# Norm seams of a two-layer hybrid backbone worked in two parts of tokens

## What is computed

```python
def _pre(x, g, mod, k):
    return _rmsnorm(x, g) * (1.0 + mod[:, 3 * k + 1][:, None]) + mod[:, 3 * k][:, None]
def _post(x, y, g, mod, k, weight):
    return x + weight * mod[:, 3 * k + 2][:, None] * _rmsnorm(y, g)
for l in range(DEPTH):
    x = _post(x, _swiglu(_pre(x, g[0], mod_lat, 0), ffn1_gu[l], ffn1_down[l]), g[1], mod_lat, 0, 0.5)
    h = _pre(x, g[2], mod_lat, 1) @ w_in[l]
    ...                                     # state-space heads and Fourier heads
    x = _post(x, y, g[3], mod_lat, 1, 1.0)
    x = _post(x, _swiglu(_pre(x, g[4], mod_lat, 2), ffn2_gu[l], ffn2_down[l]), g[5], mod_lat, 2, 0.5)
```

## Time and profile before

| | us |
|---|---|
| median of three runs (2838.31 to 2845.07) | 2840.49 |
| the profiled execution | 2843.31 |
| its span, first to last instruction | 2841.4 |
| PE busy in the span | 2729.4 |
| DVE busy | 1678.4 |
| POOL busy | 820.6 |
| ACT busy | 717.2 |

### The profile page before, as it was taken

The page is one execution under the profiler, slowest core; times in us unless marked ns, Lnnn a source line. Parts: engine busy times, 40 slices in busy tenths (PEclk is TensorE's granted clock), DMA queues, the critical chain, the costliest instruction groups (busy, mean ns, idle before and its releaser), DMA issues.

```text
span 2841.4 us, 40710 instructions
## 1 busy us (share of the span) xinstructions
PE 2729.4 (96%) x17042; PEld 2554.1 (90%) x17042; DVE 1678.4 (59%) x2235; ACT 717.2 (25%) x977; POOL 820.6 (29%) x1292
## 2 busy tenths in 40 slices
PE   5999999999999999999999899999999999999997
PEld 4899999999879899999999799999999868788886
DVE  5868876875582586766765643343344694644444
ACT  4221221112423431111111321212112424422222
POOL 1248776641050200000000226757651041100001
PEclk9899999999999999999999999999999999999999
DMA  9433444443445134344342232222323466233321
GB/s 316 126 127 129 146 137 149 125 168 98 142 149 166 52 104 127 99 131 127 110 128 82 75 72 82 90 90 86 97 86 104 162 172 191 62 97 97 97 89 60
DMA packets 340462, 337.16 MB, mean 119 GB/s; under 512 B 52528, under 2 KB 311224, under 8 KB 336696
## 3 DMA queue, kind: packets, MB, share of 16 engines
q1 hardware_dynamic: 279224, 204.07, 24.5%
q10 hardware_dynamic: 51840, 77.07, 8.1%
q0 software_dynamic: 9216, 53.42, 5.0%
HBM read 290.02 MB, written 44.50 MB: 118 GB/s over the span
## 4 chain that ended last, share of the span: by engine, by line
PE 84%; DVE 11%; ACT 2%; issue 2%; DMA 0%; POOL 0%; SPq 0%; DVEq 0%; ACTq 0%
PE ps L454 74%; DVE adaW L541 3%; PE ps L1405 2%; PE ps L582 2%; DVE tmpN L1179 1%; ACT wH L439 1%; PE ps L1098 1%; PE ps L1430 1%; DVE xT L1049 1%; DVE wL L446 1%; DVE rmsX L1188 1%; PE ps L1372 1%; PE ps L1419 1%; DMA xin<-in_x_dram 0%; PE ps L809 0%
## 5 line engine op out<-in xcount | busy, mean ns | idle before, releaser
L454 PE MATMUL ps<-hH,wH 128*128 128x384 f32 (+1 forms) x2928 | 1018.3, 348 | 18.8 <-DVE hL L1197 12.4
L454 PE MATMUL ps<-hH,wL 128*128 128x384 f32 (+1 forms) x2928 | 1011.2, 345 | 0.0
L454 PE MATMUL ps<-hL,wH 128*128 128x384 f32 (+1 forms) x2928 | 1010.8, 345 | 0.0
L446 DVE TENSOR_TENSOR wL<-raw,wH 128x1024 fp32r<-128x1024 f32 x300 | 392.6, 1321 | 536.1 <-ACT wH L439 535.7
L454 PEld LDWEIGHTS ps<-hH,wH 128*128 128x128 f32 x2928 | 555.6, 190 | 42.2 <-issue 16.9
L454 PEld LDWEIGHTS ps<-hL,wH 128*128 128x128 f32 x2928 | 555.7, 190 | 17.8
L454 PEld LDWEIGHTS ps<-hH,wL 128*128 128x128 f32 x2928 | 555.0, 190 | 18.1
L454 PE MATMUL ps<-midH,wH 128*128 128x384 f32 (+1 forms) x1232 | 426.1, 346 | 12.7 <-DVE wL L446 9.9
L454 PE MATMUL ps<-midH,wL 128*128 128x384 f32 (+1 forms) x1232 | 423.4, 344 | 0.0
L454 PE MATMUL ps<-midL,wH 128*128 128x384 f32 (+1 forms) x1232 | 423.2, 343 | 0.0
L439 ACT ACTIVATE wH<-raw 128x1024 fp32r<-128x1024 f32 x300 | 310.8, 1051 | 419.8 <-PE ps L454 399.2
(11 more groups left out here) (259 smaller groups left out, 2483.4 us busy)
## 6 DMA issues: line engine op xcount, KB each, us to landing
raw<-in_ffn_gu_dram SPq DMA_DIRECT2D x176, 512.0 KB, 3.9
adaW<-in_w_ada_dram ACTq DMA_DIRECT2D x40, 1536.0 KB, 6.9
raw<-in_ffn_down_dram SPq DMA_DIRECT2D x88, 512.0 KB, 3.5
x_d<-xT POOLq DMA_DIRECT2D x4, 3072.0 KB, 10.9
xT<-x_d POOLq DMA_DIRECT2D x4, 3072.0 KB, 10.6
W_d<-gW POOLq DMA_DIRECT2D x16, 512.0 KB, 3.8
VT_d<-gVT ACTq DMA_DIRECT2D x16, 512.0 KB, 3.0
raw<-in_w_in_dram SPq DMA_DIRECT2D x16, 512.0 KB, 5.9
```

The lines of the kernel that those rows point to most:

```text
L446: nc.vector.tensor_tensor(wL[:, n % SPLIT_SLOTS, :], raw[:, n % RAW_SLOTS, :], wH[:, n % SPLIT_SLOTS, :].bitcast(f32), ALU.subtract).then_ ...
L454: ins = nc.tensor.matmul(dst, a, b, start=first and n == 0, stop=last and n == 3 * len(pairs) - 1)
```

## The change

The tokens of a section are cut in two parts: 384 and 384, or 256 and 256 where only latent tokens are left. Part 0 holds 256 context and 128 latent tokens, part 1 only latent ones, so that its chunks take one instruction each.

- The last projection of an FFN (`last_down`) and chunks 2 to 7 of that of a mixer (`state_part`) run over part 0 first and over part 1 then. The statistics of part 0 (`post_columns`, `post_spread`) are put between the matmuls of part 1. On DVE the updates of x in part 0 stand between the additions of part 1.
- The root of the y norm needs its activation table; it is now asked for ahead of the squares (`load_root`).
- The pre-norm: rows are summed by PE as before, but copied to SBUF (`take_rows_x`), turned into columns by one-column matmuls (`pre_columns`), rooted and inverted as columns, and spread again (`pre_spread`). The root and the reciprocal of whole rows go away.
- `first_groups` takes the eight chunks of part 0 and then those of part 1. Between the matmuls of part 0 PE sums the rows of part 1.
- POOL adds chunks 0, 2 and 4 instead of 1, 3 and 5. `head_weights` of a mixer is put ahead of the last projection, and its result is taken by ACT there.
- There are fewer `keep_clock` matmuls.

The core of the diff:

```diff
 def first_groups(pe, base, count, pre):
         pe.wait_ge(w_lo, base + count)
-        for k in range(KC):
-            pe.wait_ge(h_lo, KC * pre.nth + k + 1)
-            for u in range(count):
-                wh, wl = wtile(base + u)
-                for i, (t0, w) in enumerate(halves(pre.tok0)):
+        for h, (t0, w) in enumerate(parts(pre.tok0)):
+            col = t0 - CTX if pre.tok0 else 0
+            for k in range(KC):
+                pe.wait_ge(h_lo, h_count(pre, h, k))
+                for u in range(count):
...
+                if h == 0 and pre.after:
+                    if k < 4:
+                        pre_rows(pe, pre, 1, 2 * k)
+                        pre_rows(pe, pre, 1, 2 * k + 1)
+                    elif k == 4:
+                        pre_columns(pe, pre, 1)
+                    elif k == 5:
+                        pre_spread(pe, pre, 1)
 # ffn_tensor
-        down(6 * NPH - 2, 4 + 12 * (NPH - 1), NPH - 1)
         if F.gen:
             head_weights(pe, F.gen)
+        for m in range(KC):
+            last_down(0, m)
+        last_down(1, 0)
...
+        post_columns(pe, N, 0)
+        last_down(1, 1)
+        last_down(1, 2)
+        post_spread(pe, N, 0)
+        for m in range(3, KC):
+            last_down(1, m)
+        pe.wait_ge(part_read, F.n0["part_read"] + 2 * KC)
+    def seam_tensor(pe, N, nxt):
+        keep_clock(pe, 4)
+        post_columns(pe, N, 1)
+        keep_clock(pe, 1)
+        post_spread(pe, N, 1)
+        if nxt:
+            for m in range(KC):
+                pre_rows(pe, nxt, 0, m)
+                keep_clock(pe, 1)
+            keep_clock(pe, 1)
+            pre_columns(pe, nxt, 0)
+            keep_clock(pe, 2)
+            pre_spread(pe, nxt, 0)
+            keep_clock(pe, 7)
+    def make_h(dve, pre, h, between=None):
+        for m in range(KC):
+            scale_h(dve, pre, h, m)
+            if between and m + 3 < KC:
+                between(m + 3)
+            if m >= 1:
+                rest_h(dve, pre, h, m - 1)
+        rest_h(dve, pre, h, KC - 1)
 # seam_vector, behind coef_pre and the late weight splits
+        update_x(dve, N, 1, 0)
+        update_x(dve, N, 1, 1)
+        inverse_x(dve, nxt, 0)
+        update_x(dve, N, 1, 2)
+        make_h(dve, nxt, 0, lambda m: update_x(dve, N, 1, m))
+        inverse_x(dve, nxt, 1)
+        make_h(dve, nxt, 1)
 # mix_vector, behind the additions of part 0
+        add_part(1, 2)
+        inverse_y(dve, N, 0)
+        add_part(1, 3)
+        split_lo(dve, M.base + 18)
+        update_x(dve, N, 0, 0)
+        update_x(dve, N, 0, 1)
+        add_part(1, 4)
+        update_x(dve, N, 0, 2)
+        update_x(dve, N, 0, 3)
+        add_part(1, 5)
+        split_lo(dve, M.base + 19)
+        update_x(dve, N, 0, 4)
+        add_part(1, 6)
+        update_x(dve, N, 0, 5)
+        add_part(1, 7)
 # mix_scalar
+        square_y(act, N, M, 1, 4)
+        square_x(act, N, 0, 2)
+        square_x(act, N, 0, 3)
+        square_y(act, N, M, 1, 5)
+        split_hi(act, M.base + 19)
 # start_tensor
         for R in range(FIRST_RIDES):
+            if R == 1:
+                pre_columns(pe, pres[0], 0)
+                pre_columns(pe, pres[0], 1)
+            elif R == 2:
+                pre_spread(pe, pres[0], 0)
+                pre_spread(pe, pres[0], 1)
 # start_scalar
+        take_rows_x(act, pres[0], 0)
+        take_rows_x(act, pres[0], 1)
+        split_hi(act, 0)
+        root_x(act, pres[0], 0)
+        root_x(act, pres[0], 1)
 # end_tensor: blocks 0 and 1 wait for part 0 of x only, 2 and 3 for part 1
         for b in range(4):
+            if b % 2 == 0:
+                wait_x(pe, N, b // 2, POOL_CHUNKS[-1])
+                wait_x(pe, N, b // 2, DVE_CHUNKS[-1])
+            if b == 3:
+                pe.wait_ge(s_ocp, 1)
```

More of the change, by code:

```diff
@@ L381, in build @@
     pre_first.sq = sq_first
+    pre_first.banks = (6, 7)
     F1_0 = make_ffn("f10", 0, ffn1_gu, ffn1_down, 0, 8, True)
@@ L1055, in wait_back, with add_square @@
             eng.wait_ge(x_back, 16 * N.spill)
-    def post_pool(pool, N):
-        wait_back(pool, N)
-        for m in POOL_CHUNKS:
[L1060 to L1066, removed]
+    def add_square(pool, N, h, m):
+        at = part_of(N, h)
+        pool.wait_ge(sq_y, y_count(N, h, m))
+        ins = nc.gpsimd.tensor_tensor(sumY[:, at], (sq[:, 0] if m == 1 else sumY)[:, at], sq[:, m, at], ALU.add)
+        if m < KC - 2:
+            plink(pool, ins)
+        else:
+            ins.then_inc(sum_y, 1)
@@ new lines, in build, with post_columns @@
+    STAT = 400
+    def post_columns(pe, N, h):
+        first, end = part_blocks(N.tok0, h)
+        pe.wait_ge(sum_y, 2 * N.nth + h + 1)
+        for b in range(first, end):
+            nc.tensor.matmul(ps[:, 6 + h, STAT + b:STAT + b + 1], sumY[:, b * 128:(b + 1) * 128], ones[:, 0:1],
+                             start=b == first, stop=False)
+        pe.wait_ge(sq_y, y_count(N, h, KC - 1))
+        for b in range(first, end):
+            ins = nc.tensor.matmul(ps[:, 6 + h, STAT + b:STAT + b + 1], sq[:, KC - 1, b * 128:(b + 1) * 128], ones[:, 0:1],
+                                   start=False, stop=b == end - 1)
+        ins.then_inc(ss_y, 1)
@@ L1104, in root @@
-    def root(act, bank, tok0, nth, ready, done):
-        b = tok0 // 128
-        act.wait_ge(ready, nth + 1)
-        nc.scalar.activation(sumsq[:, b:6], ps[:, bank, b:6], ACT.Sqrt, bias=ones[:, 1:2], scale=1.0 / D).then_inc(done, 1)
-    def square_y(act, N, S, m):
-        y_ready(act, S, m)
-        nc.scalar.activation(sq[:, m, N.tok0:TOK], yT[:, m, N.tok0:TOK], ACT.Square).then_inc(sq_y, 1)
-    def post_scalar(act, N, S):
-        for n in S.late:
-            split_hi(act, n)
-        root(act, 0, N.tok0, N.nth, ss_y, sd_y)
@@ new lines, in pre_columns, with pre_spread @@
+    def pre_columns(pe, pre, h):
+        first, end = part_blocks(pre.tok0, h)
+        pe.wait_ge(rows_taken, 2 * pre.nth + h + 1)
+        for b in range(first, end):
+            ins = nc.tensor.matmul(ps[:, pre.banks[h], STAT + b:STAT + b + 1], rmsX[:, b * 128:(b + 1) * 128], ident[:, 0:1],
+                                   start=True, stop=True)
+        ins.then_inc(cols_x, 1)
+    def pre_spread(pe, pre, h):
+        pe.wait_ge(rs_x, 2 * pre.nth + h + 1)
+        spread_blocks(pe, pre.tok0, h, pre.banks[h], rstdX).then_inc(bc_x, 1)
@@ new lines, in take_rows_x, with root_x @@
+    def take_rows_x(act, pre, h):
+        t0, w = parts(pre.tok0)[h]
+        act.wait_ge(rows_x, 2 * pre.nth + h + 1)
+        nc.scalar.activation(rmsX[:, t0:t0 + w], ps[:, pre.banks[h], 0:w], ACT.Copy).then_inc(rows_taken, 1)
+    def root_x(act, pre, h):
+        first, end = part_blocks(pre.tok0, h)
+        act.wait_ge(cols_x, 2 * pre.nth + h + 1)
+        nc.scalar.activation(rstdX[:, first:end], ps[:, pre.banks[h], STAT + first:STAT + end], ACT.Sqrt,
+                             bias=ones[:, 1:2], scale=1.0 / D).then_inc(sd_x, 1)
```

528 lines of the change are left out of this document (356 added, 172 removed).

## The result

The changed kernel takes 2861.19 us (median of four, 2857.76 to 2861.59) against 2840.53 before: ratio 1.0067, 95% interval 1.0055 to 1.0079. It is slower by 20.7 us, above the range. The profiled execution, with 2857.76 the shortest of the four, has a span of 2855.7, so the span grew by 14.3.

The account below looks back on a forecast made before the run. PE holds 84% of the chain, which leaves PE in the seams between sections. Start and six seams: +5.2 - 4.6 + 5.1 - 4.6 - 3.1 + 6.8 - 2.8 = +2.0, median 2842 us; range 2836 to 2848, with rivals 2827 to 2853.

Parts of the forecast that it names:

- Queues and durations: Queue-by-queue layout of instruction times; for the kernel before it gave first matmuls within 0.3 us in seams 4 and 5.
- Rival C: DVE bounds further: each additional instruction pays its whole 0.2 us and waits for its neighbour, 2.3 a seam; 2851; chance 0.26.
- The figure of the Trainium skill: Rule against the change: small DVE tiles pay fixed latency; 29 more instructions a full seam cost 4.6 us, by own figure 3.4.
- Start: Kernel start: added steps and DVE's 20.0 instead of 15.9 us for all chunks move the fourth weight unit by +5.2 us.
- Splits in the mixer's projection: Seam 2, mixer to FFN: DVE's last addition waits behind two weight splits and ends 7.4 us after PE's last matmul.
- The slow clock: Charge for half clock after PE gaps: 1.4 us each in seams 1 and 4, 2.0 in seam 2, 2.5 in seam 5.
- the link: Where a seam's measure ends: ACT's read of the first weight unit in a mixer, the fourth weight unit in an FFN.
- full-clock forecast: Seams between sections without clock charge: -6.0, +3.1, -8.0, -4.5 and +4.3 us in seams 1 to 5.
- Rival B: Gains hold and the clock stays full, as fill between rows keeps PE busier than a plain wait: -9.7, 2831; chance 0.28.
- First matmul: Sign: next section's first matmul 39 to 42 us after the last projection's start in seams 1, 3, 4; about 60 in seam 2.
- The signs: With first matmuls as early as forecast, last hL earlier than said favours full clock; later favours DVE as further bound.
- D: Rival: split additions arrive too late, first matmul stays above 52 us in FFN seams, which gain 0; 2855; chance 0.04.

Follow-up runs that it names:

- e6_link_fill: The changed kernel with more matmuls of no use in the seams' PE waits and also behind first_groups, ahead of the fourth weight unit's split: 2843.6 us.

## Why the prediction was wrong

- **Queues and durations: right.** A part 1 chunk's scale took 0.61 as assumed, the last additions in seams 1 and 2 ended at 20.5 and 42.9 (forecast 21.3 and 42.7), the spread of part 1 in seam 1 began at 24.9 (24.8). Rival C falls: DVE's part of the chain is where the layout has it, and with filled waits seams 1 and 4 come 0.7 over it, which is POOL's addition, where C had 2.3. A seam has more further DVE instructions than the 29 that I counted (seam 1 has 110 in place of 72, eight of them additions that wait for PE), so C would have cost more still. The figure of the Trainium skill (VectorE: DVE Perf Modes, The TRN2 errata) for small tiles, by which a seam would by my estimate have cost 1.2 more, is not needed either.
- **Start: right.** +5.6 against +5.2 (the last `hL` ended at 89.3, forecast 89.2), and undoing it gave 6.9 back. It was feared that the modulation steps behind it would take it up; they don't.
- **Splits in the mixer's projection: right,** in place and size: the last addition came within 0.2 of the forecast, and moving them gave seams 2 and 5 4.2 and 4.9 back.
- **The slow clock: wrong, and this is the step that failed.** I charged 1.4, 2.0, 3.4, 1.4 and 2.5 in the five seams, 10.7 in all, from the one slow stretch of the earlier trace rows, where it falls on the first matmuls, and in seam 3 from the slow clock that the kernel before had there. The trace shows it earlier as well, on columns, spread and rows, and behind the link too. Read against the full-clock forecast the seams came 3.5, 6.4, 5.9, 3.2 and 4.7 over it, 23.7. Of that 2.8 is POOL beside `hL` in four seams, which leaves some 21 for the clock, about twice the charge. That 21 is a difference and not a measurement. Filling the waits, with no other edit, gave 16.3 back in these five stretches (17.4 in the span, 18.9 in the median), so most of it is shown.
- **The diff said it.** "There are fewer `keep_clock` matmuls" was a line of the change, 57 to 23 a seam, and I priced the waits one by one, as gaps, but not that line. For the kernel before I had taken as the rule of what a gap costs, while it showed a seam whose other waits were filled.
- **Rival B** (full clock, 2831) had the size of the gains right and its condition wrong: the clock did not stay full, and its argument, that fill between rows keeps PE busier than a plain wait, is not borne out, for the same matmuls moved out of the rows left less low clock. By its sum the span would be 2831.7; the filled kernel's is 2838.3. The 48 matmuls behind the links of seams 2, 3 and 5 take 2.4, 1.6 and 1.6 longer there than at full clock (11.0, 10.1 and 12.8 against 8.6, 8.6 and 11.2 in e6_link_fill), and POOL beside `hL` takes 2.8; that is 8.4, of which 1.8 is gained elsewhere, to the 6.6 between them.
- **First matmul.** Forecast 39 to 42 us in seams 1, 3 and 4: 42.8, 44.4 and 41.4. In seam 3 1.6 of it is low clock in the projection's first matmuls, which was there before as well.
- **The signs.** A first matmul or a last `hL` later than forecast was to mean C. Both came late (64.9 and 92.5 in seam 2), but low clock moves them as well, so this sign couldn't tell C from the clock; only the fill could. And D's sum, +14.3, is by luck just the growth of the span: its condition, a first matmul above 52 in the FFN seams, isn't met.

## What to carry to other kernels

A wait on PE has two prices, its length and the half clock on what follows, and the second one depends on what else in the neighbourhood is filled; when a change thins out the matmuls that fill waits, price that line by itself. Put fill where PE waits and nowhere else: with the same 23 matmuls a seam the kernel took 14 us less when they stood in the waits than with eight of them between and behind the rows, and this half a fill was slower than none. In the kernel with all waits filled, taking the fill out from between the rows was worth some 2 us: what follows the rows waited for ACT instead, or ran at half clock. When work is cut in two so that one part runs beside the other, look first for what stands between the new pieces in an in-order queue; here two weight splits of 1.2 us in each of two seams cost 9 us.

## What the runs showed of the hardware

- Half clock came without any long wait: in seam 1 of the changed kernel it began 23.8 us after the projection's start, behind waits of 0.7 and 0.9 us and eight and twelve small matmuls. The kernel before waited 1.4 and 0.9 us between rows in the same seam and had none there. What in the work decides is not settled by these runs.
- PE was 100% busy at half clock from 708 to 712 in the changed kernel, so a busy engine is no sign that it runs at its rate. The Trainium skill (TensorE: Matmul & The Clock Gate, Part 1: The HAM clock gate) says that the low level is the default, released by activity. The runs agree in direction, with 124 us of low clock in the changed kernel and 66 in the filled one.
- A DVE instruction with both inputs in SBUF and 128 columns long took 1.09 us instead of 0.35 beside POOL's addition.
- Low clock moved between places that no edit touched, so one profiled execution tells of one seam to 2 or 3 us: the first FFN, with no edit near it, came between -0.7 and +2.7.
